# A 2-layer hybrid decoder on one core: the router turned to unnormalised rows, the experts' rows scaled on another engine, and several weight loads issued at other points

## What is computed

```python
for layer in range(DEPTH):
    hn = rms_norm(h, norm_mix[layer])
    h = h + mixer(hn)                     # two kinds
    x = rms_norm(h, norm_ffn[layer])      # h * rstd * gain
    p_grp   = softmax(x @ w_grp + b_grp)              # top 1 of 4
    e_logit = (x @ w_exp + b_exp)[chosen group]       # top 2 of 8
    h = h + sum over the 2 experts of weight * (silu(x @ w_gate[e]) * (x @ w_up[e])) @ w_down[e]
return rms_norm(h, final_norm)
```

## Time and profile before

| | |
|---|---|
| median of 3 runs | 758.96 us |
| the profiled execution | 755.92 us |
| its span, first to last instruction | 753.9 us |
| its mean granted TensorE clock | 0.942 |
| PE busy, share of the span | 634.8 us, 84% |
| DVE, ACT, POOL busy | 314.1, 225.2, 35.6 us |
| DMA moved | 246.10 MB, mean 326 GB/s |

### The profile page before, as it was taken

The page is one execution under the profiler, slowest core; times in us unless marked ns, Lnnn a source line. Parts: engine busy times, 40 slices in busy tenths (PEclk is TensorE's granted clock), DMA queues, the critical chain, the costliest instruction groups (busy, mean ns, idle before and its releaser), DMA issues.

```text
span 753.9 us, 11975 instructions
## 1 busy us (share of the span) xinstructions
PE 634.8 (84%) x4946; PEld 440.2 (58%) x4946; DVE 314.1 (42%) x536; ACT 225.2 (30%) x494; POOL 35.6 (5%) x62
## 2 busy tenths in 40 slices
PE   6998897999998675865989999999999986595775
PEld 6987786798444322413269999989954441331321
DVE  5455777446132201202275796753542211201204
ACT  5535554431121100100157675552211110110103
POOL 5100000000001100000000001060000000000000
PEclk9999999999999987978899999999999998988978
DMA  8976236469999999999997645429989999999993
GB/s 316 266 258 246 108 113 242 178 263 378 371 420 409 407 422 421 419 422 422 411 387 263 225 157 207 170 82 421 393 323 423 418 422 420 421 422 420 422 416 153
DMA packets 59506, 246.10 MB, mean 326 GB/s; under 512 B 4496, under 2 KB 8832, under 8 KB 38208
## 3 DMA queue, kind: packets, MB, share of 16 engines
q1 hardware_dynamic: 57824, 242.33, 81.7%
q0 software_dynamic: 992, 2.40, 1.0%
q10 hardware_dynamic: 640, 0.67, 0.3%
HBM read 244.34 MB, written 1.05 MB: 325 GB/s over the span
## 4 chain that ended last, share of the span: by engine, by line
PE 51%; DMA 32%; SPq 6%; DVE 5%; ACT 3%; issue 2%; DVEq 0%; ACTq 0%
DMA ring<-in_moe_w_down 30%; PE psum L1697 8%; PE psum L2114 7%; PE psum L2059 6%; PE psum L1706 5%; PE psum L1699 5%; PE psum L1708 3%; PE psum L1701 3%; SPq L488 3%; PE psum L2052 2%; DMA ring<-in_att_w_in 2%; SPq L464 2%; PE psum L1669 1%; PE psum L2043 1%; ACT w_hi L750 1%
## 5 line engine op out<-in xcount | busy, mean ns | idle before, releaser
L2059 PE MATMUL psum<-arena,xT 128*32 128x512 f32 x512 | 66.2, 676 | 38.1 <-DMA arena<-in_moe_w_up 38.1
L1438 DVE TENSOR_TENSOR arena<-psum,arena 128x256 f32<-128x256 f32 x16 | 6.8, 425 | 217.2 <-ACT arena L952 217.2
L2059 PE MATMUL psum<-ring,xT 128*32 128x512 f32 x512 | 64.5, 661 | 32.0 <-DMA ring<-in_moe_w_up 32.0
L2114 PE MATMUL psum<-ring,arena 128*32 128x512 f32 x464 | 61.9, 627 | 12.6 <-DMA ring<-in_moe_w_down 12.5
L948 ACT ACTIVATE arena<-psum 128x256 f32<-128x256 f32 x16 | 6.1, 383 | 204.6 <-PE psum L2059 204.6
L2059 PEld LDWEIGHTS psum<-arena,xT 128*32 128x32 f32 x512 | 18.1, 122 | 81.6 <-issue 46.2
L1697 PE MATMUL psum<-x_hi,w_hi 128*128 128x256 f32 x248 | 61.7, 287 | 2.1 <-DVE x_hi L1128 1.2
L750 ACT ACTIVATE w_hi<-ring 128x1024 fp32r<-128x1024 f32 x48 | 48.8, 1051 | 45.8 <-PE psum L1708 19.2
L2052 PE MATMUL psum<-arena,xg 128*128 128x128 f32 x512 | 60.3, 275 | 0.7 <-DVE arena L1425 0.7
L368 DVE TENSOR_TENSOR w_lo<-ring,w_hi 128x1024 fp32r<-128x1024 f32 x44 | 52.3, 1221 | 18.4 <-ACT w_hi L750 18.4
L2059 PEld LDWEIGHTS psum<-ring,xT 128*32 128x32 f32 x512 | 16.7, 120 | 73.9 <-issue 40.6
(11 more groups left out here) (327 smaller groups left out, 1044.8 us busy)
## 6 DMA issues: line engine op xcount, KB each, us to landing
ring<-in_moe_w_down SPq DMA_DIRECT2D x58, 1024.0 KB, 20.5
ring<-in_moe_w_gate SPq DMA_DIRECT2D x32, 1024.0 KB, 17.6
ring<-in_moe_w_up SPq DMA_DIRECT2D x32, 1024.0 KB, 19.6
arena<-in_moe_w_gate SPq DMA_DIRECT2D x32, 1024.0 KB, 22.4
arena<-in_moe_w_up SPq DMA_DIRECT2D x32, 1024.0 KB, 24.7
ring<-in_rec_w_in SPq DMA_DIRECT2D x16, 1024.0 KB, 13.9
ring<-in_att_w_in SPq DMA_DIRECT2D x8, 1024.0 KB, 11.5
ring<-in_att_w_out SPq DMA_DIRECT2D x4, 1024.0 KB, 13.8
```

The lines of the kernel that those rows point to most:

```text
L2059: return pe.matmul(bank(3)[e * CAP:(e + 1) * CAP, :].rearrange("p (w f) -> p w f", w=2), gatheredT[:, k, e * CAP:(e + 1) * CAP], w, start= ...
L2114: last = pe.matmul(bank(5 + c)[e * CAP:(e + 1) * CAP, :], hidT[:, j, e * CAP:(e + 1) * CAP], down_part(l, kind, e, j)[:, c * 512:(c + 1) * ...
```

## The change

The diff, cut to what matters:

```diff
+ROUTE_LOADED = (16 * 8, 16 * 14)
+GATHERED_PARTS = KD // 2 + 1
-        b_route = sb("b_route", [P, 1])
+        gain_ffn = sb("gain_ffn", [P, NL, KD])
+        b_route = route_t[:, 2, :, :].rearrange("p t e -> p (t e)")[:, 0:GR + NE]
...
         def load_ahead(sp, l):
             for e in range(2):
                 sp.dma_start(ahead[...], second_down(l)[e]...)
-            sp.wait_ge(s["norm_rstd"], TT * v + TT)
-            sp.dma_start(down_part(l, 1, 2, 1), ...)
-            sp.wait_ge(s["xg_done"], TT * v + TT)
-            sp.dma_start(down_part(l, 1, 2, 0), ...)
+        def load_lent(sp, l, j, *free):
+            sp.wait_ge(*free)
+            sp.dma_start(down_part(l, 1, 2, j), second_down(l)[2][:, j, :])...
...
-                free = [(s["nsa_pv"], 8), (s["sb_pv"], SB_H)] if l == 0 else [(s["a_used"], 1), (s["recT_psum"], 4)]
-                for e in range(QE):
-                    if e % 2 == 0:
-                        sp.wait_ge(*free[e // 2])
-                    load_gate_up(sp, l, 1, 1, e)
+                if l == 0:
+                    sp.wait_ge(s["nsa_pv"], 8)
+                    for e in (0, 1):
+                        load_gate_up(sp, 0, 1, 1, e)
+                    load_lent(sp, 0, 0, s["xg_done"], TT)
+                    sp.wait_ge(s["sb_pv"], SB_H)
+                    for e in (2, 3):
+                        load_gate_up(sp, 0, 1, 1, e)
+                else:
+                    load_lent(sp, 1, 0, s["rec_cum"], 2)
+                    sp.wait_ge(s["rec_qin"], 4)
+                    load_gate_up(sp, 1, 1, 1, 1, (0,))
+                    sp.wait_ge(s["ko_psum"], 4)
+                    load_gate_up(sp, 1, 1, 1, 0, (1,))
+                    sp.wait_ge(s["a_used"], 1)
+                    load_gate_up(sp, 1, 1, 1, 0, (0,))
+                    load_gate_up(sp, 1, 1, 1, 1, (1,))
+                    load_gate_up(sp, 1, 1, 1, 2, (0,))
+                    sp.wait_ge(s["recT_psum"], 4)
+                    load_gate_up(sp, 1, 1, 1, 2, (1,))
+                    load_gate_up(sp, 1, 1, 1, 3)
                 load_first(3)
+                load_ahead(sp, l)
                 sp.wait_ge(s["unit_used"], DOWN_NEEDED[l])
                 load_down(sp, l, 0)
-                load_ahead(sp, l)
+                load_lent(sp, l, 1, s["norm_rstd"], TT * (2 * l + 2))
...
@@ POOL @@
+                    for i in range(NL):
+                        pool.dma_start(gain_ffn[:, i, :], norm_ffn[i].rearrange("(p k) -> p k", k=KD))
-                pool.dma_start(b_route[0:GR, :], ...)
-                pool.dma_start(b_route[GR:GR + NE, :], ...)
+                pool.dma_start(b_route[:, 0:GR], moe_b_grp[l].partition_broadcast(P))
+                pool.dma_start(b_route[:, GR:GR + NE], moe_b_exp[l].partition_broadcast(P))
+            def route_gain(l):
+                pool.wait_ge(s["route_loaded"], ROUTE_LOADED[l])
+                pool.tensor_tensor(w_route[:, :, :], w_route[:, :, :], spread(gain_ffn[:, l, :], 2, GR + NE), ALU.mult)
             route_load(0)
-            gain_load(1)
+            route_gain(0)
...
-            pool.wait_ge(s["rec_cum"], 2)
-            gain_load(3)
...
@@ ACT, mix_and_norm @@
+                    if m == 3 and t:
+                        for half in range(TT):
+                            xT_half(v, half)
                     act.wait_ge(s["h_done"], 12 * l + i + 1)
                     link(act.activation(square_moe[:, 0:256], h[:, t, m * 256:(m + 1) * 256], ACT.Square, ...))
                     if m == 3:
...
                         rstd(v, t)
+                        if t == 0:
+                            scaled_rows(v, 0)
                 for t in range(TT):
-                    xT_half(v, t)
                     act.wait_ge(s["route_psum"], TT * l + t + 1)
                     act.activation(logit_rows[64:64 + GR + NE, ...], bank(4 + 2 * t)[64:64 + GR + NE, 0:P], ACT.Copy)
+                scaled_rows(v, 1)
+            def scaled_rows(v, t):
+                act.wait_ge(s["norm_rstd"], TT * v + t + 1)
+                act.activation(xg_parts[:, t], h[:, t, :].rearrange("p (j k) -> p k j", k=KD), ACT.Copy,
+                               scale=norm_rstd[:, v, t:t + 1]).then_inc(s["xg_done"], 1)
@@ ACT, gathered @@
-                act.activation(gatheredT[:, 0:4, :], bank(0).rearrange("p (k c) -> p k c", k=4), ACT.Copy)
+                for k in range(KD // 2):
+                    act.activation(gatheredT[:, k, :], bank(0)[:, k * P:(k + 1) * P], ACT.Copy,
+                                   scale=gain_ffn[:, l, k:k + 1])
...
@@ DVE, add_mix @@
-                    if m == 3 and t == 0:
-                        norm(v, 0)
                 xT_half(v, 0)
-                norm(v, 1)
                 xT_half(v, 1)
@@ DVE, route @@
-                    dve.tensor_scalar(logit_rows[0:GR + NE, ...], ..., b_route[0:GR + NE, 0:1], None, ALU.add)
+                    dve.tensor_copy(logit_rows[0:GR + NE, ...], bank(4 + 2 * t)[0:GR + NE, 0:P])
                 dve.wait_ge(s["route_logit"], l + 1)
+                for t in range(TT):
+                    link(dve.scalar_tensor_tensor(out=logit[:, t, :], in0=logit[:, t, :],
+                                                  scalar=norm_rstd[:, v, t:t + 1], in1=b_route[:, :],
+                                                  op0=ALU.mult, op1=ALU.add))
@@ DVE, gathered @@
-                dve.tensor_copy(gatheredT[:, 4:8, :], bank(1)...)
+                dve.tensor_tensor(gatheredT[:, 4:8, :], bank(1)..., spread(gain_ffn[:, l, 4:8], 2, P), ALU.mult)
@@ PE @@
+            def turn_rows(l, t):
+                pe.wait_ge(s["h_done"], 12 * l + MIX_ORDER[l].index((3, t)) + 1)
+                rows = h[:, t, :].rearrange("p (j k) -> p j k", k=KD)
+                for half in range(2):
+                    for k in range(4):
+                        last = pe.transpose(bank(2 * t + half)[:, k * P:(k + 1) * P], rows[:, :, 4 * half + k],
+                                            ident[:, :])
+                    last.then_inc(s["xT_psum"], 1)
@@ PE, mix_end @@
-                pe.wait_ge(s["route_loaded"], 96 * (l + 1))
-                keep_clock(NORM_MIX, 3 if l else 7)
                 for t in range(TT):
-                    transposes(2 * l + 1, t)
-                    keep_clock(TURN, 0 if t else 3 if l else 7)
+                    turn_rows(l, t)
+                pe.wait_ge(s["route_scaled"], l + 1)
+                for t in range(TT):
 ...
-                    if t == 0:
-                        keep_clock(SECOND, 7)
@@ PE, experts @@
                 route(l)
+                pe.wait_ge(s["xg_done"], TT * (2 * l + 2))
                 gather(l, 0)
```

More of the change, by code:

```diff
@@ L450, in first_units, with load_gate_up @@
                        for i, w in enumerate((wg, wu))]
-        def load_gate_up(sp, l, q, parity, e):
+        def load_gate_up(sp, l, q, parity, e, which=(0, 1)):
             half = KD * FF
-            for i, w in enumerate((moe_w_gate, moe_w_up)):
+            for i in which:
                 sp.dma_start(gate_up_slots(l, parity)[e][:, i * half:(i + 1) * half],
-                             w[l].rearrange("(q e) (p r) f -> q e p (r f)", e=QE, p=P)[q][e])\
+                             (moe_w_gate, moe_w_up)[i][l].rearrange("(q e) (p r) f -> q e p (r f)", e=QE, p=P)[q][e])\
                     .then_inc(s[f"gate_up_loaded{l}_{parity}"], 16)
@@ L596, in gain_load @@
             def gain_load(v):
[L597 to L602, removed]
+                pool.wait_ge(s[f"down{v // 2 - 1}"], 2)
+                pool.dma_start(gain[:, :], (norm_mix[1] if v == 2 else final_norm).partition_broadcast(P))\
+                    .then_inc(s["gain_loaded"], 16)
             def route_load(l):
                 if l:
-                    pool.wait_ge(s["route_used"], l)
+                    pool.wait_ge(s["passes_ready"], l)
+                else:
+                    for i in range(NL):
+                        pool.dma_start(gain_ffn[:, i, :], norm_ffn[i].rearrange("(p k) -> p k", k=KD))\
+                            .then_inc(s["route_loaded"], 16)
                 for k in (slice(0, KD // 2), slice(KD // 2, KD)):
@@ L667, in _ @@
                 .then_inc(s["lb_loaded"], 16)
+            route_gain(1)
             pool.wait_ge(s["xg_done"], 3 * TT)
@@ L941, in gathered @@
                 act.wait_ge(s[f"gathered{l}"], 2 * n + 1)
-                act.activation(gatheredT[:, 0:4, :], bank(0).rearrange("p (k c) -> p k c", k=4), ACT.Copy)\
-                    .then_inc(s["first_front" if first else f"gatheredT{l}"], 1)
+                for k in range(KD // 2):
+                    act.activation(gatheredT[:, k, :], bank(0)[:, k * P:(k + 1) * P], ACT.Copy,
+                                   scale=gain_ffn[:, l, k:k + 1])\
+                        .then_inc(s["first_front" if first else f"gatheredT{l}"], 1)
             def silu(l, n):
@@ L975, in experts @@
                 route(l)
```

(17 more changed lines are left out.)

33 lines of the change are left out of this document (17 added, 16 removed).

## The result

Five executions of each were timed together: the median after is 749.01 us (747.08 to 750.46), before 758.96 (755.74 to 759.29); ratio 0.9865, 95% interval 0.9846 to 0.9885. Forecast: 752.9, its own range 752.0 to 754 and the wide one 749.5 to 757.0, whose low end the result passes by 0.5 us. The kernel after, unchanged, was timed a second time with a later set of experiments (`after_again`): 749.87 us against 757.83, ratio 0.9906 (0.9888 to 0.9923), where I had expected 0.986 to 0.990. So the gain is 8 to 10 us, where 6.1 was forecast. The profiled execution took 747.34 us (span 745.3, mean clock 0.942), before 755.92 (753.9, 0.942): 8.6 us less.

What follows compares the result with a forecast made beforehand. PE bounds the mixers, DMA the experts. Each layer's first gather gains 4.45 us less 1.4 for strided transposes, 3.05, in all 6.1; 758.96 - 6.1 = 752.9 us, range 752.0 to 754, wide range 749.5 to 757.0.

Steps and rivals of the forecast that it cites:

- The bound and the holes: Mixers bound by PE, experts by DMA; DMA empty 3.2 and 3.4 us before the third quad's first load.
- The path without the price: Mixer's end to first gather: router's first old instruction 4.45 us earlier a layer, before any cost of strided reads.
- The price of the strided transposes: PE's 16 transposes a layer reading `h` with step 8: 1.4 us, leaving a gain of 3.05 us a layer.
- The rival that step 8 costs PE nothing: PE's strided transposes in the router: loads hide behind the products, 8.9 us gained, 750.1 us; chance 0.25.
- The queue: SP's loads in layer 0: early loads fill 163 to 168, queue empty at 179.5, before `first_used` at 186.2.
- the move: SP's queue: two 1 MB loads issued ahead of the mixer's end, so DMA finishes before the earlier `first_used`.
- the cap: If the moved loads bring nothing, DMA's hole before the third quad limits the gain to 6.6 us; chance 0.05.
- The clock: PE in the router: clock falls to half without identity products, 1.0 us a layer left, 757.0 us; chance 0.12.
- the rival: PE's clock halves in the router: products and logits' turn cost 2.1 us a layer, 757.0 us; chance 0.12.
- ACT, POOL and the mixers: Beside the path: ACT's scalings 1.0 to 2.0 us, covered; POOL's early loads cost 0; mixers unchanged at 167.5 and 153 us.
- The range: Whole kernel's time: 752.0 to 754 us with chance 0.48; 749.5 to 757.0 us holds 8 in 10.
- the free case: Step 8 costs PE's router transposes nothing: 8.9 us gained, 750.1 us; chance 0.25.

Runs made afterwards that it cites:

- after_oldqueue: The kernel after with SP's queue as before, the moved loads and both loans again behind the mixer's end; 751.89 us, ratio 0.9915 to before.
- after_noroute: The kernel after without the 19 identity products behind the logits; 754.57 us, ratio 0.9959 to before.
- before_nofill: The kernel before without the 16 identity products before and between the router's steps; 756.78 us, ratio 0.9973 to before.
- the isolated kernel: Network left out, only transposes, products and scalings at steps 1 to 16; step 8 transposes start 0.11 to 0.12 us apart, ordinary products 0.24.
- after_latescale: The kernel after with both of ACT's row scalings behind the logit copies, instead of the first ahead of row tile 1's last square; 752.77 us.

## Why the prediction was right and wrong

**The bound and the holes: right.** From `first_used` on the expert stages take 188.2 and 186.8 us before and 188.6 and 186.6 after, wherever they begin. Of the 8.5 us that the gather brings, the end gets 8.0.

**The path without the price: right to 0.25 us a layer.** 4.45 forecast, 4.2 measured. With PE's first instruction behind the mixer as zero (167.49 before, 166.87 after) the logits' turn was put at 4.43 and came at 4.35, and the router's first old instruction at 5.57 and came at 5.73: the two new instructions take 0.59 us together, not 0.46. The rest, 0.1 us, lies between it and the gather.

**The price of the strided transposes: wrong, and it is the step that failed.** "16 x 0.088 = 1.4 us" a layer; 0.06 measured. It took 1.55 ns a column from an ordinary product with step 16 (L1789) for transposes with step 8: 198 ns for the columns, and so a distance of 0.2 us. The transposes have 0.81 ns a column, 104 ns, which disappears in the distance of 0.11 us that they have packed too. (The whole load by the forecast would have been 83 + 198 = 281 ns; it measured 187.) The rival that step 8 costs PE nothing, 8.9 us and 750.1 us, is what happened: 8.5 us on the path, 749.0 to 749.9. It had 0.25, the wrong answer 0.48.

**The queue: right.** Empty at 179.5 by the forecast, the DMA's share falls from 0.81 in 178 to 180 to 0.07 behind it. Without the move the cap binds (after_oldqueue, 6.4 us), which under my own price it wouldn't have.

**The clock: not in this change, but real.** In the kernel after the granted clock is 1.00 all through the router in both profiles of it. Where PE rests for 5.4 us ahead of the gather, in after_noroute, it costs what the rival said; before_nofill shows the fall in the router itself, but no loss in its median. In the isolated kernel L104's 64 transposes with nothing between them, 7.1 us, were all granted 1.00, as were the 16 of the router. The remark of the Trainium skill that I had set beside that rival ("TensorE: Matmul & The Clock Gate", Part 4: PE-mode transpose) would have made the clock fall there; neither run shows it, in float32, where the page measured bf16.

**ACT, POOL and the mixers: right.** ACT's row scaling takes 2.15 to 2.23 us, above the upper bound of 2.0, and is covered all the same; the second ends at 173.3, the gather starts at 178.7. The router's weights are multiplied at 41.1 us, long before 167. The second mixer is 155.0 us as before; the first mixer's difference can't be told from its spread.

**The range** ended 0.5 us too high. Of the 3.9 us between 752.9 and 749.01 the price makes 2.7, less 0.5 by which the path fell short; the other 1.7 the two profiles don't show. Its lower end was the free case less 0.6 us. The median of before that it started from was itself 0.6 to 1.1 us above the medians of the same kernel in the three sets of experiments (758.35, 757.83, 758.21 us), and the time after moved by as much between sets. The range had left that out.

## What to carry to other kernels

A transpose may read its rows with a step where an ordinary product may not: price an access pattern by a row of the same kind of instruction that reads it, and look at the distance between starts before a longer load is called a cost. An earlier consumer is paid out only up to the hole in the transfers that it opens, so read the hole's length before counting on the gain; moving loads into another hole pays only together with it. Identity products that hold the clock can go where the work has closed up; where PE would rest for 5.4 us ahead of the gather, leaving them out cost 4.7 us.

## What the runs showed of the hardware

- 16 fp32 transposes of 128x128: 1.8, 2.0, 2.0, 1.8, 1.9 us with steps 1, 2, 4, 8, 16. Ordinary fp32 products with a stationary of step 8: 0.24 us a record instead of 0.11, and with a moving operand of step 8, 0.22.
- ACT on 128x1024 fp32: 1.06 us packed, 1.18 with step 2, 2.0 to 2.1 with steps of 4 to 16.
- Around rests of 1.04 and 0.39 us ahead of the first gather the clock fell to 0.50 in some layers of some executions and not in others with the same rests (after_latescale: layer 0 yes, layer 1 no). What decides it is open.
